# Two tiles are added on VectorE ahead of one product with ones, in four group norms and in a convolution's norm

## The reference, cut to what matters

```python
y = y.reshape(bsz, seq, SSD_WIDTH) * jax.nn.silu(z.astype(jnp.float32))
yg = y.reshape(bsz, seq, g, SSD_WIDTH // g)          # 4 groups of 256
yg = yg * lax.rsqrt(jnp.mean(yg * yg, axis=-1, keepdims=True) + EPS)
```

```python
h = causal_dwconv_2(h, dw) + dw_b                    # 256 channels
return jax.nn.silu(layer_norm_2(h, ln_g, ln_b))
```

## Time and profile before

| what | value |
|---|---|
| three runs | 3341.06, 3343.58 and 3345.88 us, median 3343.58 |
| the profiled execution | 3341.49 us |
| its span, first to last instruction | 3339.4 us |
| what lies around the span | 2.1 us |
| mean granted TensorE clock | 0.999 |
| PE busy | 3294.9 us, 99% of the span |
| DVE busy | 2286.0 us, 68% |
| ACT busy | 1522.5 us, 46% |

### The profile page before, as it was taken

One profiled execution on the slowest core, in us unless ns is written; L12 is line 12 of the kernel. 1 busy time (PEld: TensorE's weight loads), 2 busy tenths in 40 slices (PEclk: granted clock), 3 DMA queues, 4 the chain that ended last, 5 costly groups with the idle time before them and its releaser, 6 DMA issues.

```text
span 3339.4 us, 46683 instructions
## 1 busy us (share of the span) xinstructions
PE 3294.9 (99%) x17322; PEld 2785.5 (83%) x17322; DVE 2286.0 (68%) x3629; ACT 1522.5 (46%) x2450; POOL 252.7 (8%) x302
## 2 busy tenths in 40 slices
PE   8999999999999999999999999999999999999999
PEld 6878887888888889878888898889887788888897
DVE  5777876478876767678654677567656875457574
ACT  4455434344444444445744444344434575444343
POOL 1000000000000000028200000000000670000000
PEclk9999999999999999999999999999999999999999
DMA  4333332232333333322221333333332232223332
GB/s 146 90 88 89 107 99 94 89 113 93 101 101 89 94 100 102 87 89 89 89 89 55 97 101 97 96 98 101 93 106 83 88 102 76 76 76 93 108 100 78
DMA packets 424782, 314.15 MB, mean 94 GB/s; under 512 B 15432, under 2 KB 421376, under 8 KB 424592
## 3 DMA queue, kind: packets, MB, share of 16 engines
q1 hardware_dynamic: 421264, 301.77, 30.2%
q0 software_dynamic: 2896, 8.49, 0.8%
q10 hardware_dynamic: 432, 1.38, 0.1%
HBM read 309.46 MB, written 2.13 MB: 93 GB/s over the span
## 4 chain that ended last, share of the span: by engine, by line
PE 88%; DVE 4%; issue 3%; POOL 3%; ACT 1%; DMA 0%; DVEq 0%; SPq 0%; POOLq 0%; ACTq 0%
PE G L790 63%; PE B L839 7%; PE G L839 6%; POOL arena L3269 2%; PE G L1029 2%; PE G L1006 2%; PE B L779 1%; PE G L731 1%; PE B L710 1%; PE B L1029 1%; PE B L682 1%; PE G L1051 1%; DVE w_lo L2310 1%; PE G L1069 1%; PE G L779 0%
## 5 line engine op out<-in xcount | busy, mean ns | idle before, releaser
L1453 ACT ACTIVATE w_hi<-raw 128x1024 fp32r<-128x1024 f32 x421 | 445.8, 1059 | 877.5 <-PE G L790 797.1
L2310 DVE TENSOR_TENSOR w_lo<-raw,w_hi 128x1024 fp32r<-128x1024 f32 x422 | 521.8, 1237 | 441.2 <-ACT w_hi L1453 439.3
L790 PE MATMUL G<-y_hi,w_hi 128*128 128x512 f32 x1824 | 720.7, 395 | 0.3 <-DVE w_lo L2310 0.2
L790 PE MATMUL G<-y_hi,w_lo 128*128 128x512 f32 x1824 | 710.4, 389 | 0.0
L790 PE MATMUL G<-y_lo,w_hi 128*128 128x512 f32 x1824 | 710.0, 389 | 0.0
L790 PE MATMUL G<-xn_hi,w_hi 128*128 128x512 f32 x1504 | 591.8, 393 | 0.8 <-DVE w_lo L2310 0.8
L790 PE MATMUL G<-xn_hi,w_lo 128*128 128x512 f32 x1504 | 585.6, 389 | 0.0
L790 PE MATMUL G<-xn_lo,w_hi 128*128 128x512 f32 x1504 | 585.4, 389 | 0.0
L790 PEld LDWEIGHTS G<-y_hi,w_hi 128*128 128x128 f32 x1824 | 342.5, 188 | 80.4 <-issue 9.0
L790 PEld LDWEIGHTS G<-y_lo,w_hi 128*128 128x128 f32 x1824 | 342.5, 188 | 73.8 <-issue 4.3
L790 PEld LDWEIGHTS G<-y_hi,w_lo 128*128 128x128 f32 x1824 | 342.4, 188 | 71.9
(11 more groups left out here) (546 smaller groups left out, 5865.9 us busy)
## 6 DMA issues: line engine op xcount, KB each, us to landing
raw<-in_w_in SPq DMA_DIRECT2D x128, 512.0 KB, 4.4
raw<-in_ffn_w_gate SPq DMA_DIRECT2D x88, 512.0 KB, 4.0
raw<-in_ffn_w_up SPq DMA_DIRECT2D x88, 512.0 KB, 5.2
raw<-in_ffn_w_down SPq DMA_DIRECT2D x64, 512.0 KB, 4.3
raw<-in_w_mlp_up SPq DMA_DIRECT2D x32, 512.0 KB, 4.6
raw<-in_w_mlp_down SPq DMA_DIRECT2D x32, 512.0 KB, 4.3
raw<-in_xa_wkv SPq DMA_DIRECT2D x32, 512.0 KB, 4.3
raw<-in_w_out SPq DMA_DIRECT2D x24, 512.0 KB, 4.3
```

The costliest lines, as they stand in the source:

```text
L790: m = pe.matmul(bank[:, 0:n], a[:, k, kt, :], b[:, kt * S:kt * S + n], start=(kt == tiles[0] and t == 0), stop=(kt == tiles[-1] and t == 2))
L1453: act.activation(weights_part(w_hi, n + 1, k), raw_part(n + 1, k), ACT.Copy).then_inc(s_whi, 1)
L2310: dve.tensor_tensor(weights_part(w_lo, n + 1, k), raw_part(n + 1, k), weights_part(w_hi, n + 1, k).bitcast(F32), ALU.subtract).then_inc(s_ ...
```

## The change: what it does

Each of the eight places with two float32 products with ones (four groups, and mean and variance in two layers) keeps one. VectorE adds the two tiles first, with one TENSOR_TENSOR of 128x512 float32. For a group the add (`group_squares` on VectorE) stands in the next pair, right behind the first `prep_lo`; for the mean it stands in VectorE's step 19, behind the selection; for the variance it is the last instruction of `mean()`, linked to (waiting for) the second square. TensorE waits for the add in place of what it waited for before.

```diff
             def sums(step):
                 bank = take(("cln", l, step), (conv_v, ("stat", l, step)), sums_in)
-                for k in range(2):
-                    if step:
-                        pe.wait_ge(conv_v.sem, conv_v.at("summand", l, step, k))
-                    else:
-                        pe.wait_ge(conv_p.sem, conv_p.at("add", l, adds["conf", CONV_TAPS - 1, k]))
-                    m = pe.matmul(bank[:, :], ones, cv[k] if step == 0 else tmp(4 + k), start=k == 0, stop=k == 1)
-                m.then_inc(full.sem, full.mark("cln", l, step))
+                pe.wait_ge(conv_v.sem, conv_v.at("summand", l, step))
+                pe.matmul(bank[:, :], ones, tmp(4), start=True, stop=True).then_inc(full.sem, full.mark("cln", l, step))
...
             def group_sums(g):
                 bank = take(("zsum", g), (z_v, ("var", g)))
-                for k in range(2):
-                    pe.wait_ge(z_a.sem, z_a.at("square", g, k))
-                    m = pe.matmul(bank[:, :], ones, tmp(k), start=k == 0, stop=k == 1)
-                m.then_inc(full.sem, full.mark("zsum", g))
+                pe.wait_ge(z_v.sem, z_v.at("squares", g))
+                pe.matmul(bank[:, :], ones, tmp(0), start=True, stop=True).then_inc(full.sem, full.mark("zsum", g))
...
                     link(dve.tensor_tensor(cv[k], cv[k], stat[:, :], ALU.subtract))
-                    dve.tensor_tensor(tmp(4 + k), cv[k], cv[k], ALU.mult).then_inc(conv_v.sem, conv_v.mark("summand", l, 1, k))
+                    ins = dve.tensor_tensor(tmp(4 + k), cv[k], cv[k], ALU.mult)
+                link(ins)
+                dve.tensor_tensor(tmp(4), tmp(4), tmp(5), ALU.add).then_inc(conv_v.sem, conv_v.mark("summand", l, 1))
...
+                if i == mean_step - 1:
+                    for k in range(2):
+                        dve.wait_ge(conv_p.sem, conv_p.at("add", l, adds["conf", CONV_TAPS - 1, k]))
+                    dve.tensor_tensor(tmp(4), cv[0], cv[1], ALU.add).then_inc(conv_v.sem, conv_v.mark("summand", l, 0))
                 if i == mean_step + 1:
                     mean()
...
+            def group_squares(g):
+                for k in range(2):
+                    dve.wait_ge(z_a.sem, z_a.at("square", g, k))
+                dve.tensor_tensor(tmp(0), tmp(0), tmp(1), ALU.add).then_inc(z_v.sem, z_v.mark("squares", g))
...
                     prep_lo(n, q, k)
+                    if i and k == 0:
+                        group_squares(i - 1)
...
                     if (i, k) == (0, 0):
+                        group_squares(3)
                         group_norm(2)
```

## The result

The changed kernel takes 3349.06 us in the median (22 runs, 3343.86 to 3351.8), the kernel before 3343.61 us (22 runs, 3340.7 to 3346.01): ratio 1.0016, interval 1.0010 to 1.0022, 5.45 us more. That is inside the range and within 0.2% of before, on the slow side, as forecast; the likeliest time, 3347.2 us, was 1.9 us too low. The execution profiled took 3344.94 us, so it is one of the quicker ones (only one of the 22 was quicker) and shows less than the median does.

The account below looks back on a forecast made before the run. PE, busy for 99% of the span, was taken as the bound. Groups -3.44, mean +4.30, variance -0.28 and clock +3.02 give +3.60 us, 3347.2 us against the median, range 3341 to 3351: no measurable change.

Parts of the forecast that it names:

- the range: Whole kernel: 3341 to 3351 us, from the in-between case to two more clock falls than the forecast's two.
- The price of a product: One float32 product with ones holds PE for 0.86 us; eight removed give at most 6.88 us.
- The groups: Group norms in phase `z`: adds hidden in VectorE's waits, four products saved, -3.44 us.
- The mean: Step 0 of the convolution's sums: PE waits 3.17 us for the late add, net +2.15 us per layer.
- The variance: Step 1 of the sums: scores before it wait 0.72 us more, product saves 0.86, -0.14 us per layer.
- The clock: Behind the mean's new wait PE's clock falls in both layers, 1.51 us each, +3.02 us.
- The rival of several spells: Clock stays at 1.2 GHz for several spells behind each new wait; three per layer give +9.6 us, 3353.2 us; chance 0.07.
- The sum without the clock: Whole kernel if the clock does not fall at the mean's waits: +0.58 us.
- The bound "-0.86 us per layer" for a hidden mean: Mean's sum: if its wait were hidden after all, the removed product would give -0.86 us per layer.

Follow-up runs that it names:

- the groups alone: Only the four group norms changed, the convolution's norm as in the kernel before: 3337.88 us against 3343.44, ratio 0.9988.
- the filled kernel: The whole change plus three products with ones on PE in front of the mean's wait: 3342.77 us, ratio 0.9999 to the kernel before.
- the mean alone: Only the convolution's mean changed against the kernel before, its add behind the selection: 3353.88 us, ratio 1.0037.
- the variance alone: Only the variance changed against the kernel before, its add linked behind the second square: 3342.83 us against 3343.66, ratio 0.9997.
- both moved: The whole change with the mean's add in VectorE's step 18 and the variance's behind step 22's maximum: 3340.36 us against 3343.66 before, ratio 0.9990.
- the mean's add early: The whole change with the mean's add in VectorE's step 18, before the split of the weights: 3339.37 us, ratio 0.9989 to the kernel before.

## Why the prediction was right, and where it was off

- **The price of a product** (0.86 us): right, 12.65 - 11.78 = 0.87 us a pair in phase `z`.
- **The groups** (-3.44 us, adds hidden): right, by the period, by the missing wait and by the lowest levels of the groups alone. That VectorE needs longer than PE for a pair shows as the lost 0.80 us of waiting and reaches nothing.
- **The mean** (+2.15 us a layer without the clock, wait of 3.17 us): right. The wait was 3.28 us, and from scores to scores the filled kernel takes 1636.83 - 1629.58 = 7.25 us where 5.21 is the untouched value: +2.04 us.
- **The variance** (-0.14 us a layer): right, 0.69 us lost in front of the sum (0.72 was said) and 0.86 saved by it, -0.17 us.
- **The clock** (1.51 us in each layer, 3.02 together) is the term that was mis-sized. It fell at both waits, as the forecast took it. That agrees with what the Trainium skill, which the forecast named, says of a wait that is long enough (TensorE: Matmul & The Clock Gate, "HAM oscillation — how this bites in real kernels"); that 3.17 us would be long enough was the forecast's own step, from the rows of the 2.61 us waits. But its price was taken from one spell at the lower clock in each layer. Here it measured 1.20 and 2.57 us in the profiled execution, 3.8 together, and in the medians the whole change and the filled one differ by 3349.06 - 3342.77 = 6.3 us; a part of that can lie at the 2.61 us waits, whose falls differ from one profile to the next. The rival of several spells was so half right: the stretch at the lower clock was 6.8 us in one layer of the change and in both of the mean alone. Its reason, that small products follow the wait, isn't needed: the last section shows the same 6.8 us at 2.61 us waits, with half a panel behind them.
- **The sum without the clock** (+0.58 us): the filled kernel's median has it at -0.7 us, its interval holding both. The rows above add up to 4 x -0.87 + 2 x (2.04 - 0.17) = +0.3 us.
- **The bound "-0.86 us per layer" for a hidden mean** was wrong: hidden, it gives 0, since VectorE's selection bounds the next scores. The rows of before already had it: the `maximum` behind the selection starts at 1637.65, and the scores, at 1638.36, come right behind its end.
- **The range** held the median only because its upper end had two more falls of the clock in it; the rival to which such falls belong, several spells at a wait, had a chance of 0.07.

So of the 6.9 us that eight products are worth, 3.4 came in with the groups. The convolution's 3.4 were turned into waits, and the clock at the mean's cost more than the groups saved.

## What to carry to other kernels

Work moved off the busiest engine pays only where the other engine's place for it is early enough: look up in the timeline where that engine stands when the product is due, before the price of the product. And it pays only where the busiest engine's next work isn't waiting for that other engine anyway: the mean's product gave nothing until VectorE's `maximum` was moved as well. A wait of TensorE can cost the lower clock on top of its length: here 1.20 and 2.57 us on top of some 2 us that the late sum lost. Products that nobody reads, put into a wait that can't be removed, gave that part back here. And where runs gather at levels, compare like levels or traces, since a few runs' medians can differ by a whole level.

## What the runs showed of the hardware that was not expected

The spread of the runs of the kernel before, 3340.4 to 3346.7 us, is for the most part TensorE's clock: with two waits of 2.61 us filled it is 3338.7 to 3341.8. And behind the same wait of 3.28 us, with the same work to follow, the granted clock was 0.50 for the stretch of 3.4 us shown in one layer and for 6.8 us in the other, in one execution. The longer stretch comes at 2.61 us waits too: here in the variance alone (first layer) and in both moved (second layer), the scores that end the wait, and the windows.

```profile
1582.25 0.80 PE L642 MATMUL B<-arena 64*128 64x128 f32 x4 [2.61 <-DVE small L2185]
...
2709.28 0.80 PE L642 MATMUL B<-arena 64*128 64x128 f32 x4 [2.61 <-DVE small L2176]
```

```profile
1581.90:1588.70 6.80, 6.45 (x31) 6.26 (x32) 2.00 (x7) 2.76 (x10) 1.71 (x3) 0.50 0.19 65
2708.70:2715.50 6.80, 6.22 (x29) 6.03 (x30) 2.24 (x9) 2.99 (x10) 1.95 (x3) 0.50 0.21 72
```

In the profiles of the eleven kernels the clock fell 15 times at a wait of 2.61 or 3.28 us, 11 of them at the 16 unfilled waits of 2.61 us. In five of the 15 it went down 0.35 us or more before the wait ended, and these lasted 6.8 us; in the other ten it went down at most 0.23 us before the end, or up to 1.6 us behind it, and these lasted 3.4 us. So here the price hung on when the fall came against the end of the wait. What sets that moment no run tests.

Twice the clock fell behind no wait at all, in the mean alone at 2575.6 and in the mean's add early, where PE was busy for all of the 6.9 us before:

```profile
1430.00:1436.90 6.90, 6.90 (x34) 4.95 (x33) 5.78 (x12) 2.76 (x6) 0.00 (x0) 1.00 0.01 2
1436.90:1440.40 3.50, 3.50 (x10) 2.69 (x9) 2.02 (x4) 0.00 (x0) 0.00 (x0) 0.51 0.92 294
```

One thing stays open: the kernel with only the mean's wait filled had its eleven runs within 1.8 us (3341.2 to 3343.0), though its 2.61 us waits were not filled; in its profile the clock is down behind the second layer's (granted 0.50 from 2712.2 to 2715.6) and not behind the first's.
